# The expert weights of a routed feed-forward block in transfers of 2 MB with rows of 16 KB

## The reference, cut to what matters

```python
def one_group(hs):
    logits = jnp.einsum('ld,de->le', hs, w_router, preferred_element_type=jnp.float32)
    aff = jax.nn.softmax(logits, axis=-1)
    g, idx = lax.top_k(aff.T, cap)
    xg = hs[idx]
    a = jnp.einsum('ecd,edf->ecf', xg, w_gate)
    u = jnp.einsum('ecd,edf->ecf', xg, w_up)
    y = jnp.einsum('ecf,efd->ecd', jax.nn.silu(a) * u, w_down)
    y = y * g[..., None].astype(y.dtype)
    out = jnp.zeros((L, D), y.dtype).at[idx.reshape(-1)].add(y.reshape(-1, D))
    return out.astype(hs.dtype)
```

## Time and profile before

| | |
|---|---|
| median of three runs | 1775.61 us (1772.8 to 1778.5) |
| the profiled execution: its own time | 1778.93 us |
| the profiled execution: its span, first to last instruction | 1777.1 us |
| TensorE busy, matmuls | 1522.3 us (86%) |
| VectorE, ScalarE, GpSimd busy | 591.8, 386.1, 132.4 us |
| moved by DMA | 511.49 MB, mean 288 GB/s |
| mean granted TensorE clock | 0.965 of 2.4 GHz |

### The profile page before, as it was taken

The page is one execution under the profiler, slowest core; times in us unless marked ns, Lnnn a source line. Parts: engine busy times, 40 slices in busy tenths (PEclk is TensorE's granted clock), DMA queues, the critical chain, the costliest instruction groups (busy, mean ns, idle before and its releaser), DMA issues.

```text
span 1777.1 us, 18601 instructions
## 1 busy us (share of the span) xinstructions
PE 1522.3 (86%) x7789; PEld 880.0 (50%) x7789; DVE 591.8 (33%) x984; ACT 386.1 (22%) x688; POOL 132.4 (7%) x135
## 2 busy tenths in 40 slices
PE   7998899988778778778788787698798989979999
PEld 7674433322222222222222222496696778968887
DVE  6473200101001001000010010577773754768843
ACT  5332000000000000000000000355231445345532
POOL 1010000000000000000000000101430340410000
PEclk9998899999999999999999999799898989989999
DMA  9335899999999999999999999352231324445564
GB/s 385 123 127 219 331 415 418 416 415 415 419 416 415 415 419 416 414 417 418 415 415 418 417 415 415 145 189 84 83 109 41 119 83 154 155 142 173 187 197 142
DMA packets 99731, 511.49 MB, mean 288 GB/s; under 512 B 9521, under 2 KB 9777, under 8 KB 64705
## 3 DMA queue, kind: packets, MB, share of 16 engines
q1 hardware_dynamic: 97888, 506.12, 72.8%
q10 hardware_dynamic: 1760, 4.19, 0.7%
HBM read 509.23 MB, written 1.05 MB: 287 GB/s over the span
## 4 chain that ended last, share of the span: by engine, by line
PE 47%; DMA 37%; DVE 9%; POOL 3%; ACT 2%; issue 2%; SPq 0%; ACTq 0%; DVEq 0%; POOLq 0%
DMA sb_ring<-in_w_up 22%; DMA sb_ring<-in_w_gate 13%; PE PS L755 7%; PE PS L674 6%; PE PS L1103 6%; PE PS L712 5%; PE PS L772 3%; PE PS L791 2%; PE PS L691 2%; DVE sb_wp L1920 2%; PE PS L584 2%; PE PS L864 2%; PE PS L771 1%; DMA sb_raw<-in_w 1%; PE PS L474 1%
## 5 line engine op out<-in xcount | busy, mean ns | idle before, releaser
L674 PE MATMUL PS<-sb_ring,sb_XG 128*64 128x512 f32 x2048 | 485.7, 602 | 112.0 <-DMA sb_ring<-in_w_up 55.9
L674 PEld LDWEIGHTS PS<-sb_ring,sb_XG 128*64 128x64 f32 x2048 | 133.4, 136 | 458.3 <-issue 169.6
L1939 DVE TENSOR_TENSOR sb_SL<-sb_SL,PS 128x512 f32<-128x512 f32 x32 | 20.5, 683 | 811.8 <-PE PS L674 811.8
L712 PE MATMUL PS<-sb_ring,sb_HT 128*64 128x512 f32 x1024 | 234.5, 607 | 30.1 <-DMA sb_ring<-in_w_down 15.5
L1920 DVE TENSOR_TENSOR sb_wp<-sb_raw,sb_wp 128x1024 fp32r<-128x1024 f32 x160 | 202.1, 1266 | 112.5 <-ACT sb_wp L1292 111.0
L1292 ACT CAST sb_wp<-sb_raw 128x1024 fp32r<-128x1024 f32 x160 | 167.2, 1046 | 149.4 <-PE PS L1103 56.3
L755 PE MATMUL PS<-sb_hr,sb_wp 128*128 128x256 f32 x1440 | 189.2, 294 | 6.1 <-DVE sb_hr L1970 3.4
L755 PEld LDWEIGHTS PS<-sb_hr,sb_wp 128*128 128x128 f32 x1440 | 183.9, 201 | 9.6 <-issue 5.9
L712 PEld LDWEIGHTS PS<-sb_ring,sb_HT 128*64 128x64 f32 x1024 | 80.8, 139 | 173.5 <-issue 110.0
L1304 ACT ACTIVATE sb_SL<-PS 128x512 f32<-128x512 f32 x32 | 17.4, 595 | 517.7 <-PE PS L674 517.7
L772 PE MATMUL PS<-sb_hr,sb_wp 128*128 128x512 f32 x256 | 89.1, 401 | 3.4 <-DVE sb_hr L1970 3.4
(11 more groups left out here) (391 smaller groups left out, 1388.1 us busy)
## 6 DMA issues: line engine op xcount, KB each, us to landing
sb_ring<-in_w_gate SPq DMA_DIRECT2D x128, 1024.0 KB, 24.6
sb_ring<-in_w_up SPq DMA_DIRECT2D x128, 1024.0 KB, 26.5
sb_ring<-in_w_down SPq DMA_DIRECT2D x128, 1024.0 KB, 21.0
sb_raw<-in_w SPq DMA_DIRECT2D x160, 512.0 KB, 3.8
sb_ring<-in_w_in SPq DMA_DIRECT2D x12, 1024.0 KB, 16.0
sb_ring<-in_w_out SPq DMA_DIRECT2D x4, 1024.0 KB, 12.9
sb_KW<-in_kw SPq DMA_DIRECT2D x1, 1403.0 KB, 18.0
sb_H<-in_x ACTq DMA_DIRECT2D x2, 512.0 KB, 5.0
```

The lines of the kernel that those rows point to most:

```text
L674: ins = e.matmul(PS[64 * g:64 * g + 64, b, :], m.XG[:, k, r0:r0 + 64], m.ring[s][:, (2 * g + q) * 512:(2 * g + q) * 512 + 512], start=(k = ...
L712: ins = e.matmul(PS[64 * g:64 * g + 64, b, :], m.HT[:, c % 8, (c // 8) * 64:(c // 8) * 64 + 64], m.ring[s][:, a * 1024 + g * 512:a * 1024 ...
```

## The change

Buffers 2j and 2j + 1 of the ring now form one region of 2 MB, `ring_pair[j]`; `ring[s]` are its halves, at the addresses that they had. The host lays gate and up side by side: `w_gate_up[ex, k]` is 128 rows of 4096 numbers (16 KB), 2048 of gate and 2048 of up. `w_down[ex, s]` holds four rows of down behind each other per partition, also 16 KB, and the whole of such a pair is contiguous in memory. A new function `fetch_pair` waits until both pieces that were there are used up and issues one transfer for the pair; its completion is counted on the even buffer's semaphore, and `brought` tells TensorE to wait for the even piece of the pair. Two pairs are still brought in halves, 8 KB of each row at a time, with a wait for each: pieces 28 and 29 (expert 0), whose buffers come free at different times in the attention, and the last two of all, 398 and 399. What is computed, its order on TensorE and where each number lies in SBUF stay as they are.

```diff
+HALVED = (28, 16 + 24 * 16 - 2)
...
-        self.ring = [sb(f"ring{s}", ring0 + 2048 * s, 2048) for s in range(RING)]
+        self.ring_pair = [sb(f"ring{s}", ring0 + 4096 * s, 4096) for s in range(RING // 2)]
+        self.ring = [self.ring_pair[s // 2][:, 2048 * (s % 2):2048 * (s % 2) + 2048] for s in range(RING)]
...
+def brought(i):
+
+    return i if i - i % 2 in HALVED else i - i % 2
...
             for mat in range(2):
                 slot = expert_slot(ex, 2 * k + mat)
                 s = ring_slot(slot)
-                pe.wait_ge(*at("w", slot))
+                pe.wait_ge(*at("w", brought(slot)))
...
         for s8 in range(8):
             slot = expert_slot(ex, 16 + s8)
             s = ring_slot(slot)
-            pe.wait_ge(*at("w", slot))
+            pe.wait_ge(*at("w", brought(slot)))
...
-        dst = m.ring[s] if len(src.shape) == 2 else m.ring[s].rearrange("p (a d) -> p a d", a=src.shape[1])
-        e.dma_start(dst, src).then_inc(*mark(f"ring{s}", "w", i, by=16))
+        e.dma_start(m.ring[s], src).then_inc(*mark(f"ring{s}", "w", i, by=16))
+
+    def fetch_pair(i, src):
+
+        if i in HALVED:
+            fetch(i, src[:, 0:2048])
+            fetch(i + 1, src[:, 2048:4096])
+        else:
+            s = ring_slot(i)
+            for event in freed(i) + freed(i + 1):
+                sp.wait_ge(*at(*event))
+            e.dma_start(m.ring_pair[s // 2], src).then_inc(*mark(f"ring{s}", "w", i, by=16))
...
     for ex in range(NE):
         for k in range(8):
-            fetch(expert_slot(ex, 2 * k), t["w_gate"][ex, k * 128:k * 128 + 128, :])
-            fetch(expert_slot(ex, 2 * k + 1), t["w_up"][ex, k * 128:k * 128 + 128, :])
-        for s in range(8):
-            fetch(expert_slot(ex, 16 + s), t["w_down"][ex, 256 * s:256 * s + 256, :].rearrange("(a p) d -> p a d", p=128))
+            fetch_pair(expert_slot(ex, 2 * k), t["w_gate_up"][ex, k])
+        for s in range(4):
+            fetch_pair(expert_slot(ex, 16 + 2 * s), t["w_down"][ex, s])
...
-    for n in ("w_gate", "w_up", "w_down"):
-        a[n] = np.ascontiguousarray(i[n][0])
+    a["w_gate_up"] = np.concatenate([i[n][0].reshape(NE, 8, 128, 2048) for n in ("w_gate", "w_up")], 3)
+    a["w_down"] = np.ascontiguousarray(i["w_down"][0].reshape(NE, 4, 4, 128, D).transpose(0, 1, 3, 2, 4)).reshape(NE, 4, 128, 4 * D)
```

## The result

| | before | after |
|---|---|---|
| median | 1776.63 us (4 runs) | 1752.01 us (4 runs) |
| lowest to highest | 1772.8 to 1778.5 us | 1750.9 to 1757.55 us |
| ratio, with its 95% interval | | 0.987 (0.9843 to 0.9897) |
| span of the profiled execution | 1777.1 us | 1750.1 us |

What follows compares the result with a forecast made beforehand. The prediction took the DMA stream of expert weights to bound the kernel; -18.0 us for rows and +1.0 us for the start gave -17.0 us, from 1775.61 to 1758.6 us, range 1750 to 1771 us (0.8).

Steps and rivals of the forecast that it cites:

- The saving for the rows: Weight stream: 16 KB rows mean fewer packets at 7.4 ns each, saving 1.18 us an expert, 18.0 us in all.
- better end: Weight stream: upper bound with no fixed cost for a 16 KB row, 1.89 us an expert, 1748 us; chance 0.05.
- The rest of 0.42 us in an expert: Each expert's 60.75 us is 0.42 us over its pieces' 60.33 us, put down to instruction packets and assumed unchanged.
- The start, +1.0 us: Stream start near 190 us: waiting for two pieces costs 1.8 us, less a 0.84 us loss that goes away.
- that loss goes away: The 0.84 us lost in the stream's next 10 us, at 384 GB/s instead of 419, would vanish with pairs.
- Waits for room later on: Later in the stream, waiting for two pieces of room costs nothing while transfers queue: 6 of 20 pieces needed.
- TensorE's waits for a pair: On TensorE, the gate half is used 2.5 us later, 1.94 us more lag an expert, caught up in down: nothing.
- The last pair in halves: End of the stream: halving the last pair leaves only 1 MB of matmuls after the last landing, so no cost.
- A: Rival for the stream: fixed cost half as large or ending at 8 KB, 6.3 us saved, 1769 us; chance 0.14.
- B: Rival: the stream doesn't gain, only the start's +1.0 us is left, 1776.6 us; chance 0.11.
- C: Rival for the stream: 16 KB packets move no faster than the slowest steady ones, +15 us, 1791 us; chance 0.10.
- D: Rival: each transfer pays its own cost, one after another, an estimated 380 us less here; given no chance.

Runs made afterwards that it cites:

- the kernel with halves there: The changed kernel with the stream's first six pairs after the ring was full (36 to 46) brought in halves: 1749.74 us, ratio 0.9851.
- The kernel with four pieces of room too early: The changed kernel with 32 KB rows (4 MB transfers) from mid expert 1 to expert 14 and pairs 36 to 46 in halves: 1751.83 us.
- the second pair of traces: Both kernels run and traced again with nothing changed: 1751.62 us for the changed kernel (four runs), 1772.36 us for the kernel before (one run).

## Why the prediction was right, and by how much it was off

- **What bounds the stage.** Right. With pairs landing 4.903 us apart and TensorE still waiting 1.25 us for each, every step followed the landings, and the kernels with faster landings ended the stage earlier.
- **The saving for the rows.** The mechanism was right, a fixed cost for each packet; its size was the term that failed. "0.059 us / 8 = 7.4 ns" rested on the difference of 2.494 and 2.553 us, where an error of 0.01 us is 1.3 ns, and on packet counts that gave the same. From 8 KB up it is some 10 ns. Measured steps give 8 x (4.988 - 4.903) + 4 x (5.106 - 4.903) = 1.49 us an expert instead of 1.18, and 22.7 us in all instead of 18.0. The "better end" had covered it: 1.89 us.
- **The rest of 0.42 us in an expert,** left as it is. That was sound. The first trace after has 59.10 - 12 x 4.903 = 0.26 us, but that hangs on which expert one ends with: between experts 7 and 11 it is (839.15 - 602.25) / 4 = 59.22 us an expert, a rest of 0.39. Most experts take 58.8 us, which is twelve pairs and nothing else (before, 60.3), and three to five of the twelve take 0.5 us or more longer. What delays those isn't shown.
- **The start, +1.0 us.** Too small: 1.3 to 2.3 us by the kernel with halves there. The step that failed is "that loss goes away": the first 10 us still ran at 370 GB/s and the next 20 at 411. It isn't the pairs that hold the first 10 us down, since the kernel with halves has 365 GB/s in them; 411 instead of its 422 in the next 20 is what pairs cost beyond the first wait. Why the first 10 us are slow isn't shown: a pair comes free every 4.78 us, which would allow 439 GB/s.
- **Waits for room later on, TensorE's waits for a pair, its clock, SyncE: nothing.** Right, at a DMA share that stays over 1. The kernel with four pieces of room too early shows the limit, and with clock 0.95 and pauses of 2.6 us nothing was lost either.
- **The last pair in halves, counted as needed.** Wrong, without effect on the sum: ScalarE's order hid it.
- **The sum.** 22.7 less 1.3 to 2.3 is 20.4 to 21.4 us, against 21.1 and, in the second pair of traces, 1118.48 - 1098.98 = 19.5 us at the last down matmul, 18.8 to 20.5 us at the second block's first. So the forecast of 17.0 was 2 to 4 us short for what the change does, and the medians add 4 us from the second block, which the forecast didn't foresee and which no part of the change is shown to make. That the two errors, 4.7 us too little for the rows and up to 1.3 us too little for the start, partly cancel is luck.
- **The rivals.** A falls: gate and up gained 0.085 us a pair. The 3.5 ns of the Trainium skill, DMA: Bandwidth & Descriptors, section "Why small descriptors are slow (HBM only)", are a third of the 9 to 10 ns measured. B and C fall with the same steps: a packet of 16 KB takes 612.9 ns, and the 0.92 us of the instruction queue's said nothing of it. B's two blocks for one transfer also fall with the kernel of 2 MB in rows of 8 KB. D has 5 ns for a transfer on each engine, less than a packet's.

## What to carry to other kernels

When the transfers themselves bound a stretch, lay the data out on the host so that each partition's row is one contiguous run as long as the buffers allow, and take the gain from the steps between landings: here 10 ns for each packet and next to nothing for the size of a transfer. By the last down matmul, rows of 8 KB for down (1109.09 us) gave 9 to 10 us, rows of 16 KB throughout another 10 to 11, and rows of 32 KB (1093.54 us) another 4 to 5. Larger transfers are not free where the queue is thin: at the start of a stream each waits for all of its room, and small ones there give that back. Before crediting a change with what a profile shows, compare the part that it doesn't touch: here 6 us of 27 came and went with the clock, and compare two traces of the same kernel before reading one landing to the microsecond.

## What the runs showed of the hardware that was not expected

- Two transfers of 64 partitions instead of one of 128 halve the rate: 215 GB/s instead of 428, with all 16 engines busy at 1.22 us for a packet of 16 KB instead of 0.61. The kernel took 2541.9 to 2626.93 us.
- Rows of 32 KB go as one packet each, 1.215 us, at 431 GB/s.
- With rows of 16 KB a transfer lands 45.2 us after its issue, 18 MB deep, where it was 21 to 26 us and 8 to 10 MB: with 18 of the ring's 20 MB in flight, its room may be the limit there. It isn't the size of the transfers alone: those of 2 MB in rows of 8 KB land 32.9 us after their issue. What bounds the depth isn't shown. The depth had no effect on the rate.
- At one second block, with nothing changed in it, the traces differ by up to 7 us (627.5 to 634.5 us), and with them the time that TensorE spent at its lower clock (51 to 68 us).
